# A two-block transformer kernel: the order of VectorE's and ScalarE's work ahead of and inside the mLSTM slots of the second block

## What is computed

```python
def step(carry, xs):                       # one chunk of tokens
    C, n, m = carry
    b = jnp.cumsum(fc, axis=-1)            # fc, ic: log gates
    d_intra = jnp.where(causal, b[..., :, None] - b[..., None, :] + ic[..., None, :], -jnp.inf)
    d_prev = b + m[..., None]
    m_t = jnp.maximum(d_prev, jnp.max(d_intra, axis=-1))
    s = jnp.einsum('bhtd,bhsd->bhts', qc, kc) * jnp.exp(d_intra - m_t[..., None])
    num = jnp.exp(d_prev - m_t)[..., None] * jnp.einsum('bhtd,bhde->bhte', qc, C) + jnp.einsum('bhts,bhse->bhte', s, vc)
    qn = jnp.exp(d_prev - m_t) * jnp.einsum('bhtd,bhd->bht', qc, n) + jnp.sum(s, axis=-1)
    h = num / jnp.maximum(jnp.abs(qn), jnp.exp(-m_t))[..., None]
    ...                                    # C, n and m of the next chunk
```

## Time and profile before

| what | value |
|---|---|
| median of 3 runs | 3512.49 us (3503.08 to 3513.25) |
| profiled execution | 3517.86 us, its span 3515.8 us |
| mean granted clock of TensorE | 0.973 |
| busy: TensorE, GpSimd, VectorE, ScalarE | 96%, 51%, 45%, 35% |
| second block, layer 0: tiles and slots ahead of the neighbourhood attention | about 1708 to 1956 us |
| the same, layer 1 | about 2767 to 2971 us |

### The profile page before, as it was taken

The page is one execution under the profiler, slowest core; times in us unless marked ns, Lnnn a source line. Parts: engine busy times, 40 slices in busy tenths (PEclk is TensorE's granted clock), DMA queues, the critical chain, the costliest instruction groups (busy, mean ns, idle before and its releaser), DMA issues.

```text
span 3515.8 us, 49684 instructions
## 1 busy us (share of the span) xinstructions
PE 3391.0 (96%) x17334; PEld 2792.9 (79%) x17334; DVE 1591.3 (45%) x2511; ACT 1214.6 (35%) x1967; POOL 1783.8 (51%) x2019
## 2 busy tenths in 40 slices
PE   8999999999999999999899999999999899999998
PEld 6778887887768887887788877888888787878887
DVE  4542257776634237777645443311212554442112
ACT  4433342223433232223433453321212334443222
POOL 5325567776425557779444223333434454246555
PEclk9999999999999999999899999999999999999999
DMA  4212234443212234444332112111111332132222
GB/s 168 81 48 97 96 131 175 166 167 133 105 49 78 101 114 171 161 168 153 115 99 82 49 49 96 55 60 66 60 63 62 109 112 75 55 114 99 98 96 102
DMA packets 105265, 358.39 MB, mean 102 GB/s; under 512 B 11873, under 2 KB 20321, under 8 KB 103201
## 3 DMA queue, kind: packets, MB, share of 16 engines
q1 hardware_dynamic: 70560, 257.13, 20.7%
q10 hardware_dynamic: 34560, 99.30, 8.2%
HBM read 336.79 MB, written 8.59 MB: 98 GB/s over the span
## 4 chain that ended last, share of the span: by engine, by line
PE 79%; DVE 8%; issue 7%; ACT 3%; POOL 1%; ACTq 1%; DMA 0%; DVEq 0%; POOLq 0%; SPq 0%
PE ps L966 8%; PE ps L965 8%; PE ps L967 8%; PE ps L662 5%; PE ps L663 5%; PE ps L664 5%; PE ps L907 3%; PE ps L908 3%; PE ps L909 3%; PE ps L1033 3%; PE ps L1034 2%; PE ps L1035 2%; PE ps L686 2%; DVE ada_junk L2147 2%; PE ps L687 2%
## 5 line engine op out<-in xcount | busy, mean ns | idle before, releaser
L547 POOL TENSOR_TENSOR w_lo<-w_raw,w_hi 128x256 fp32r<-128x256 f32 x1904 | 1663.8, 905 | 1673.2 <-ACT w_hi L1363 1659.7
L1363 ACT ACTIVATE w_hi<-w_raw 128x1024 fp32r<-128x1024 f32 x472 | 499.2, 1058 | 851.3 <-PE ps L967 349.2
L662 PE MATMUL ps<-h_hi,w_hi 128*128 128x512 f32 x944 | 374.5, 397 | 0.0
L663 PE MATMUL ps<-h_lo,w_hi 128*128 128x512 f32 x944 | 370.0, 392 | 0.0
L664 PE MATMUL ps<-h_hi,w_lo 128*128 128x512 f32 x944 | 370.0, 392 | 0.0
L1033 PE MATMUL ps<-c_hi,w_hi 128*128 128x512 f32 (+1 forms) x832 | 305.1, 367 | 19.9 <-DVE vm L2296 11.9
L2147 DVE SCALAR_TENSOR_TENSOR ada_junk<-ada_w,c_silu 128x1024 f32<-128x1024 f32 x192 | 307.3, 1601 | 3.3
L1034 PE MATMUL ps<-c_lo,w_hi 128*128 128x512 f32 (+1 forms) x832 | 292.6, 352 | 0.0
L1035 PE MATMUL ps<-c_hi,w_lo 128*128 128x512 f32 (+1 forms) x832 | 291.6, 351 | 0.0
L965 PE MATMUL ps<-c_hi,w_hi 128*128 128x512 f32 (+1 forms) x768 | 274.8, 358 | 5.7 <-DVE c_lo L2262 5.7
L966 PE MATMUL ps<-c_lo,w_hi 128*128 128x512 f32 (+1 forms) x768 | 275.2, 358 | 0.0
(11 more groups left out here) (353 smaller groups left out, 6192.1 us busy)
## 6 DMA issues: line engine op xcount, KB each, us to landing
w_raw<-in_w SPq DMA_DIRECT2D x476, 512.0 KB, 3.5
ada_w<-in_ada ACTq DMA_DIRECT2D x96, 512.0 KB, 5.2
zs<-stage ACTq DMA_DIRECT2D x52, 128.0 KB, 2.1
m_row<-m_spill ACTq DMA_DIRECT2D x16, 384.0 KB, 5.4
wq_row<-wq_spill ACTq DMA_DIRECT2D x16, 384.0 KB, 5.5
x_spill<-x ACTq DMA_DIRECT2D x2, 2048.0 KB, 7.6
zs_m<-zm ACTq DMA_DIRECT2D x32, 128.0 KB, 2.1
bias<-in_rpb ACTq DMA_DIRECT2D x8, 512.0 KB, 3.9
```

Of the source, the lines that this page charges most:

```text
L547: last = nc.gpsimd.tensor_tensor(w_lo[:, j, c], w_raw[:, j % RAW, c], w_hi[:, j, c].bitcast(F), ALU.subtract)
L662: nc.tensor.matmul(bank, w_hi[:, j, w], rhs_hi[:, k, :], start=(k == 0), stop=False)
L663: nc.tensor.matmul(bank, w_hi[:, j, w], rhs_lo[:, k, :], start=False, stop=False)
L1363: nc.scalar.activation(w_hi[:, j, :], w_raw[:, j % RAW, :], ACT.Copy).then_inc(hi_ready, 1)
```

## The change

On ScalarE, `keys_by_token(0)` moves from behind the six row loads to between `gate_maxima` and `gate_decays`. The loads of slot 1's maxima (`load_maxima(L, 1, first)`) go behind tile 4 and the query weights' loads. On VectorE, tile 3 moves from behind `gate_sums` to behind the second scan of maxima. In the slots, `query_weights` becomes two functions, called ahead of `weigh`; a tile that is not turned is taken ahead of both, and a tile that is turned (`ROTATED`) is taken behind `weigh`.

```diff
@@ attention, ScalarE @@
                 gate_maxima(L)
+                keys_by_token(0)
                 gate_decays(L)
                 act.wait_ge(m_stored, (L + 1) * 32)
                 load_maxima(L, 0, first)
-                load_maxima(L, 1, first)
+                take(4)
                 act.wait_ge(wq_stored, (L + 1) * 32)
                 load_query_weights(0)
-                keys_by_token(0)
-                take(4)
+                load_maxima(L, 1, first)
                 gate_columns(L)
@@ gate_sums, VectorE @@
-            def gate_sums(L, between):
+            def gate_sums(L, between, values):
...
-                def scans(dst, first_op, second_op, one, src, step):
+                def scans(dst, first_op, second_op, one, src, step, between=None):
                     n = CTX
                     nc.vector.tensor_tensor_scan(dst[fw, :], one(fw, ALL), src[fw, :], 0.0, first_op, second_op)
                     nc.vector.tensor_tensor_scan(dst[bw, C][:, ::-1], one(bw, n), src[bw, C][:, ::-1], 0.0, first_op, second_op).then_inc(gate_v, 1)
+                    if between:
+                        between()
...
-                scans(run_m, ALU.max, ALU.max, lambda rows, n: same[n](rows), key_w, 7)
+                scans(run_m, ALU.max, ALU.max, lambda rows, n: same[n](rows), key_w, 7, values)
@@ mlstm, VectorE @@
-                def query_weights(v):
+                def forward_queries(v):
                     hp, f, n, t0, c = slot(v, first)
                     if f == 0:
                         dve.wait_ge(wq_loaded[hp % 2], (L * 2 + hp // 2 + 1) * 32)
                     if v >= 2:
                         dve.wait_ge(mi_ready, L * SLOTS + v - 1)
                     nc.vector.tensor_tensor(q_w[:, f, 0:n * P], qm[:, hp, c], wq_row[hp % 2][:, 0, c], ALU.mult)
+
+                def backward_queries(v):
+                    hp, f, n, t0, c = slot(v, first)
                     dve.wait_ge(ms_ready, L * SLOTS + v + 1)
                     nc.vector.tensor_tensor(qm[:, hp, c], qm[:, hp, c], wq_row[hp % 2][:, 1, c], ALU.mult).then_inc(qw_ready, 1)
...
-                    take(FILLS[v][0] - 1, L, g0, first)
+                    turned_now = FILLS[v][0] - 1 in ROTATED
+                    if not turned_now:
+                        take(FILLS[v][0] - 1, L, g0, first)
+                    forward_queries(v)
+                    backward_queries(v)
                     weigh(v)
-                    query_weights(v)
+                    if turned_now:
+                        take(FILLS[v][0] - 1, L, g0, first)
@@ the calls, VectorE @@
-                gate_sums(L, lambda: take(2, L, g0, first))
-                for p in range(3, FILLS[0][0] - 1):
+                gate_sums(L, lambda: take(2, L, g0, first), lambda: take(3, L, g0, first))
+                for p in range(4, FILLS[0][0] - 1):
```

## The result

| | before | after |
|---|---|---|
| median us (runs) | 3512.87 (3503.08 to 3516.82, 4) | 3473.55 (3464.70 to 3474.13, 4) |
| ratio | 1 | 0.9886, interval 0.987 to 0.9901 |
| profiled execution, span | 3517.86, 3515.8 | 3464.70, 3462.7 |
| granted clock of the span | 0.973 | 0.983 |

The change makes the kernel 39.3 us faster by the medians. Measured once more, it gave 42.6 (experiment 5). The profiled execution of after was the fastest of its four, so the two traces differ by 53.1 us; I therefore compare stretches, not spans. The stretch from the first projection tile behind the gates to the first matmul of the neighbourhood attention took 247.41 us in layer 0 before and takes 221.25 (1706.83 to 1928.08), and 204.26 and 184.40 (2734.95 to 2919.35) in layer 1. That is 26.16 + 19.86 = 46.0 us by the traces, against 47.3 predicted.

The account below looks back on a forecast made before the run. TensorE, busy 96% of the span, bounds the kernel; its waits also bring half clock. Terms 9.0 (ahead of slots) + 17.1 (slot waits) + 21.2 (clock) = 47.3 us, giving a median of 3465.2, stated as 3466; range 3452 to 3492.

Parts of the forecast that it names:

- The forecast case: Whole kernel: the full sum of 47.3 us, or within 8 us of it, is gained; chance 0.62.
- 17.1 us of waits: Slots of both layers: cross products' waits for weighted queries removed, 17.1 us, between 14 and 19.9.
- The clock was to give back 21.2: Slots of both layers: half-clock stretches behind removed waits return to full clock, saving 21.2 us.
- the dip in slot 7 of layer 1 (3.0 us), which the sum kept: Half-clock stretch in slot 7, layer 1: expected to stay; its 3.0 us counted only in the low end.
- Rival 1: Slots: half clock belongs to the small matmuls and stays; gain 26 us, 3486 us; chance 0.17.
- Rival 2: Slots: TensorE waits for the weighting instead, or ScalarE's weights and GpSimd's masking cannot follow; 3491 us; chance 0.13.
- Rival 3: Slots: short pauses everywhere cost TensorE the full clock in every slot; slower, 3529 us; chance 0.04.
- Rival 4: Slots: forward queries are not ready early, held by row loads or previous cross products; within 0.3%; chance 0.04.
- For both layers 9.0 us: Ahead of the slots: additions start earlier, limited by GpSimd, by 6.6 us in layer 0 and 2.4 in layer 1.
- with 3.85 us of masking and 2.97 us of values the additions start at 1753.2: Ahead of layer 0's slots: maxima rows land at 1746.4, then GpSimd's masking and values set the additions' start; gain 6.6 us.
- this wait goes: Ahead of layer 0's slots: copying the first value tile earlier removes TensorE's 6.21 us wait for it.
- The bounds of that step, 5.7 to 11.0: Ahead of the slots: gain 5.7 us if a row load's issue is held up, 11.0 if GpSimd's rows land no later.

Follow-up runs that it names:

- experiment 5: The changed kernel measured once more, unaltered: 3471.99 us, ratio 0.9875 against the kernel before.
- experiment 1: Changed kernel with ScalarE's order and the first value tile put back as before, so only the slots are changed: 3465.14 us, ratio 0.9854 against before.
- experiment 3: Changed kernel with every tile, turned or not, taken first and the queries still ahead of the weighting: 3488.30 us, ratio 0.9916 against before.
- experiment 6: Changed kernel with GpSimd making the weighted values of pair 0 before masking slot 0's maxima rows: 3465.64 us, ratio 0.9852 against before.
- experiment 11: Changed kernel with ScalarE's order as before; ahead of the slots only the value tile is early: 3473.37 us, one run.
- experiment 12: Changed kernel with VectorE's gate work as before; ahead of the slots only ScalarE's new order: 3465.23 us, one run.
- experiment 8: Changed kernel with seven extra copies of the forward multiply between scores and backward multiply in every slot: 3614.52 us, ratio 1.0279 against before.
- experiment 10: Changed kernel with four extra copies of the forward multiply in every slot: 3555.99 us, ratio 1.0109 against before.
- experiment 2: Changed kernel with the slots' order put back as before, so only the part ahead of the slots is changed: 3514.12 us, ratio 0.9998 against before.
- experiment 4: Changed kernel with the queries back behind the weighting; only a turned tile goes last: 3487.26 us, ratio 0.9919 against before.
- experiment 7: Experiment 6's kernel with VectorE also taking the output gates (slots 3, 6, 7) behind the weighting: 3463.04 us, ratio 0.985 against before.
- experiment 9: Experiment 7's kernel with ScalarE taking tile 5 ahead of slot 0's weights: 3455.66 us, ratio 0.9825 against before.

## Why the prediction was right, and where it missed

**The forecast case came true.** The predicted 3466 us lies 7.6 below the median of 3473.55, and the gain was 46.0 by the traces' stretches and 39 to 43 by medians (35 to 46 by the interval), against 47.3. That 46.0 comes so near to 47.3 is in part luck: 4.6 too much ahead of the slots stand against 0.6 too little for the waits in them and 2.7 too little for the clock.

**In the slots: right.** 17.1 us of waits were to go; 11.3 + 8.6 - 0.93 - 1.24 = 17.7 went. The clock was to give back 21.2; the stretches give 46.0 - 4.4 - 17.7 = 23.9. All seven dips are gone, slot 1's by the amounts predicted. The difference is about the dip in slot 7 of layer 1 (3.0 us), which the sum kept. That it went is chance: the same wait of 1.24 or 1.25 us had no dip behind it in the changed kernel and in experiment 5, and had one in experiments 1, 3, 6, 11 and 12. Rival 1 (the half clock belongs to the small matmuls) falls: the same small matmuls run at 1.00 with no wait ahead of them, and at 0.55 when experiment 8 puts one there; in the 14 kernels here, none of the 140 slots without a wait of L1309 has a dip. Rival 2 in the slots falls too: L1318 waits 0.2 us in all. Rival 3 needed waits everywhere, and there are none. Rival 4 fell with the first row of VectorE above.
The Trainium skill (TensorE: Matmul & The Clock Gate, Why this matters for your kernels) warns only of longer idle gaps, and by it the dips behind short waits would have had another cause. The traces don't bear that out: waits of 1.23 to 1.53 us, put there by experiment 10, had half clock behind them.

**"For both layers 9.0 us" ahead of the slots: too high, 4.4 by the traces and nothing that medians resolve.** The failed step is "with 3.85 us of masking and 2.97 us of values the additions start at 1753.2". Against that sum, in layer 0:
- The gate chain was only 0.33 us later, not 1.02: the third maximum scan took 1.27 us in place of 1.57 and a difference 0.95 in place of 1.36. The same operation on the same tile is not a fixed price.
- The rows landed 7.57 us after their issue began, not 6.28. Why is open. In the seven kernels where the swap of tile 4's rows was issued while they were on their way it was 7.6 to 8.5; in experiment 12, where the swap came 5.4 us behind them, 6.6; in before and experiments 1 and 11, where it came after they had landed, 6.2 to 6.3. The prediction had moved that swap and asked only who waits for it. No run moved it alone.
- The masking took 4.80 us, not 3.85. It does so in every kernel here whose turn of tile 4 lies beside it (4.77 to 4.83 in the changed kernel and experiments 2 to 10 and 12), and 3.85 or 3.86 us in before and in experiments 1 and 11, where the turn came later. Layer 1 shows it in steps: 2.80 or 2.81 us with no instruction of VectorE beside it (experiments 1 and 11), 3.26 or 3.27 with one step of the turn beside it in full (before and experiments 3 and 4), and 3.71 to 3.81 with two (the changed kernel and experiments 2, 5, 8 and 10). I had moved that turn in my working and looked only at who waits for its result, not at what runs beside it. That these two engines share something is inferred from this and from the multiply that ended when GpSimd's row of operations did (experiment 3); no run took the turn away alone.
- So the additions waited 4.53 us, and what I had used in every slot held here as well: at half clock they took 1.3 us longer than before, and in layer 1, behind 2.04 us, 1.2. The forecast's own mechanism was at work there, and I had priced it only inside the slots.

**The early value tile** was counted as a removed wait of 5.7 to 6.2 us a layer. It was not on the path of layer 0: whatever TensorE gains there it waits out at L1254 or L1288, which are set by ScalarE's and GpSimd's chains (experiments 11 and 12). The sum had this right, as it priced the front by GpSimd; the words "this wait goes" would have misled on their own.

**The bounds of that step, 5.7 to 11.0,** did not hold the 4.4. The lower one was made from a held-up issue, and no issue was held up; the masking's own duration and the clock of the additions, which moved, had no bounds.

**The spread.** Half-clock time also falls in stages that no variant touches. A wait of 1.83 us of L1004 behind the slots of layer 0 had half clock behind it in before and in experiments 3, 6 and 9, and none in the changed kernel and experiments 1, 4 and 5. Over 13 runs of the kernel before, time and mean granted clock go together with a correlation of -0.93: 3500.28 us at 0.977, 3525.30 at 0.971. That is 2 x 0.006 x 3510 = 42 us more at half clock for 25 us. So two profiled executions can differ by 7 us outside of the change, as they did here.

## What to carry to other kernels

Price a wait of TensorE together with the granted clock of the stretch behind it: here 17.7 us of waits carried 23.9 us of slow matmuls, and a comparison of two equal stretches gave slot 1's share to 0.2 us. Where a wait is removed ahead of a join, follow every chain into the join and give the new wait its dip as well. And when an operation is moved, ask also what it will now run beside: a key tile's turn, moved to where it was free, lay beside another engine's work on the path, and that work took longer.

## What the runs showed of the hardware

- **The length of a wait doesn't decide alone.** Slot 4 of layer 0 waited 1.55 us in before and ran at 1.00 behind it; in the front-only kernel it waited 1.54 us and fell to 0.64. The two stretches, of before and of the front-only kernel:

```profile
1858.07:1864.07 6.00, 6.00 (x53) 1.00 0.00 1
```

```profile
1856.65:1862.65 6.00, 6.00 (x42) 0.64 0.00 0
```

  With queries first, slot 1 waited 1.78 us with no dip behind it; with the turn last, slot 3 waited 0.91 us and had one (below), where the same wait in before had none. Over the 224 slots of the 14 kernels here: none of the 140 without a wait of L1309 had a dip, all of the 38 waits from 1.80 us on had one, and of the 46 waits between 0.15 and 1.78 us 18 had one, the shortest of them 0.59 us (with another 0.62 of L1318 right behind it). One of those 18 is among the 16 waits up to 0.80 us, the other 17 are among the 30 from 0.85 us on. What decides in the single case stays open.

```profile
1830.92 0.89 PE L1309 MATMUL ps<-state,q_w 64*128 64x65 f32 x12 [0.91 <-DVE qm L2432]
...
1833.00:1840.00 7.00, 7.00 (x36) 0.51 0.02 8
```

- **The price of half clock** was 0.41 and 0.43 us of longer busy time for each us of it (experiments 8 and 10), not 0.5. Part of it falls where TensorE stands anyway: of the 6.85 us at half clock around the additions of layer 0 (1750.80 to 1757.65) it was busy for 4.66.
- **A transfer's way from issue to landing** isn't fixed by its size: the same pair of row loads took between 6.2 and 8.5 us from the start of their issue in these kernels.
- **Two-input operations of VectorE and GpSimd lengthen each other.** A multiply of 128 x 256 on VectorE took 0.42 us in slot 1 of layer 1 and 3.58 to 7.96 us in slot 0, each time ending 0.27 or 0.28 us after a row of GpSimd's operations that stood back to back (the changed kernel and experiments 3, 5, 8 and 10). What they share, these traces don't say.
